# A fused two-block kernel: order of TensorE's work in the linear-attention mixer, by token tile

## The reference

```python
def gla_mixer(u, w_in, w_gk2, b_gk, g_norm, w_out):      # 4 heads, dk 128, dv 256, chunks of 64 tokens
    q, k, v, g, gk_lr = jnp.split(u @ w_in, [...], axis=-1)
    log_a = jax.nn.log_sigmoid((gk_lr @ w_gk2 + b_gk)) / GLA_GATE_TAU
    ...
    cum = jnp.cumsum(to_chunks(log_a, GLA_DK_HEAD), axis=3)
    e_pos = jnp.exp(cum)
    e_neg = jnp.exp(-cum)
    q_fwd = qc * e_pos
    a_fwd = jnp.einsum('bhntd,bhnsd->bhnts', q_fwd, kc * e_neg)
    a_bwd = jnp.einsum('bhntd,bhnsd->bhnts', qc * e_neg, kc * e_pos)
    o_intra = jnp.einsum('bhnts,bhnsv->bhntv', jnp.where(lower, a_fwd, a_bwd), vc)
    k_to_end = kc * jnp.exp(cum[:, :, :, -1:, :] - cum)
    chunk_decay = jnp.exp(cum[:, :, :, -1, :])

    def step(state, inp):
        qs, ke, vv, dec = inp
        o = jnp.einsum('bhtk,bhkv->bhtv', qs, state)
        state = state * dec[..., None] + jnp.einsum('bhtk,bhtv->bhkv', ke, vv)
        return state, o
    ...
    o = o_intra + o_inter
    o = o * lax.rsqrt(jnp.mean(jnp.square(o), -1, keepdims=True) + RMS_EPS) * g_norm
    return (o * jax.nn.silu(g)) @ w_out
```

## Time and profile before

| what | value |
|---|---|
| device time, median of 3 runs | 1047.37 us (1047.06 to 1048.85) |
| the profiled execution, device time | 1045.79 us |
| its span | 1043.8 us |
| its mean granted clock of TensorE | 0.992 |
| TensorE, VectorE, ScalarE busy | 97%, 62%, 19% of the span |
| bytes read from HBM | 203.64 MB, 196 GB/s over the span |

### The profile page before, as it was taken

The page is one execution under the profiler, slowest core; times in us unless marked ns, Lnnn a source line. Parts: engine busy times, 40 slices in busy tenths (PEclk is TensorE's granted clock), DMA queues, the critical chain, the costliest instruction groups (busy, mean ns, idle before and its releaser), DMA issues. The chain is left out here.

```text
span 1043.8 us, 12930 instructions
## 1 busy us (share of the span) xinstructions
PE 1010.2 (97%) x4878; PEld 712.5 (68%) x4880; DVE 652.4 (62%) x1533; ACT 203.1 (19%) x492; POOL 26.3 (3%) x53
## 2 busy tenths in 40 slices
PE   7999999999999999899999999999999999999994
PEld 4858755858755757656777777668886677777762
DVE  2786644785642341546899888975332577766668
ACT  4134214134212231202000000022223110001000
POOL 2000000000000000000001000001000000000000
PEclk9999999999999999999999999999999999999997
DMA  9954457754447355173669877825433345554411
GB/s 357 379 175 181 169 172 272 291 194 158 180 166 297 137 221 207 42 293 115 231 248 344 299 249 266 289 85 205 149 131 121 121 140 183 206 184 175 162 40 41
DMA packets 29909, 205.50 MB, mean 197 GB/s; under 512 B 3630, under 2 KB 3795, under 8 KB 6172
## 3 DMA queue, kind: packets, MB, share of 16 engines
q1 hardware_dynamic: 27116, 191.60, 50.4%
q0 software_dynamic: 2736, 13.11, 3.3%
HBM read 203.64 MB, written 1.05 MB: 196 GB/s over the span
## 5 line engine op out<-in xcount | busy, mean ns | idle before, releaser
L1503 PE MATMUL bank<-hT,raw 128*128 128x256 f32 x1056 | 235.1, 382 | 2.0 <-DMA raw<-units_dram 2.0
L1503 PEld LDWEIGHTS bank<-hT,raw 128*128 128x128 f32 x1056 | 200.1, 191 | 33.6 <-issue 3.8
L1792 PE MATMUL bank<-yT,arena 128*128 128x512 f32 x224 | 100.8, 593 | 0.0
L1792 PE MATMUL bank<-raw,arena 128*128 128x512 f32 x180 | 86.8, 593 | 0.0
L1792 PEld LDWEIGHTS bank<-yT,arena 128*128 128x128 f32 x224 | 42.5, 190 | 53.9 <-issue 51.7
L820 DVE CUSTOM_DVE_ANT_0 raw<-raw,crow 128x1024 f32<-128x1024 f32 x64 | 75.3, 1220 | 0.2 <-DVEq L118 0.2
L1816 PEld LDWEIGHTS bank<-hT,raw 128*128 128x128 f32 x448 | 54.3, 192 | 12.4 <-issue 12.4
L1513 PE MATMUL bank<-raw,hT 128*128 128x512 f32 x128 | 55.4, 592 | 0.0
L676 ACT ACTIVATE arena<-bank 128x512 f32<-128x512 f32 x28 | 16.7, 597 | 197.0 <-PE bank L1816 197.0
L1816 PE MATMUL bank<-hT,raw 128*128 128x128 f32 x448 | 54.5, 275 | 0.0
L1513 PE MATMUL bank<-raw,yT 128*128 128x512 f32 x112 | 49.5, 596 | 2.1 <-DVE yT L1432 2.0
(11 more groups left out here) (342 smaller groups left out, 1398.8 us busy)
## 6 DMA issues: line engine op xcount, KB each, us to landing
raw<-units_dram SPq DMA_DIRECT2D x180, 1024.0 KB, 4.8
arena<-ln_rows_dram POOLq DMA_DIRECT2D x4, 1024.0 KB, 5.5
arena<-att_line_dram POOLq DMA_DIRECT2D x4, 512.0 KB, 6.0
arena<-small_dram POOLq DMA_DIRECT2D x2, 896.0 KB, 7.1
arena<-ada_rows_dram POOLq DMA_DIRECT2D x1, 1536.0 KB, 8.0
xt<-x_dram SPq DMA_DIRECT2D x2, 512.0 KB, 4.5
arena<-post_g_dram POOLq DMA_DIRECT2D x2, 512.0 KB, 8.8
kst<-consts_dram SPq DMA_DIRECT2D x1, 608.0 KB, 15.9
```

The costliest lines, as they stand in the source:

```text
L1503: mm = pe.matmul(b[:, c * S:(c + 1) * S], raw[:, s, k * 256 + c * P:k * 256 + (c + 1) * P], act_t[:, k, :], start=(k == 0), stop=(k == KC ...
L1792: return pe.matmul(SB[i][:], x, y, start=False, stop=stop)
```

## The change

On TensorE alone, three things are done in the GLA mixer. The key transposes stand ahead of the scores. The waits ahead of the outputs are split by token tile: tile 0 waits for `st0_ready` 2 and `att_ready` 2, tile 1 for `att_ready` 4 and `st_ready` 8. And the output units wait apart: the first for `yg_ready` 4, the second for `yg_ready` 8. No instruction with work in it is added or removed, and the programs of the other engines are the same.

```diff
@@ -1921,6 +1921,11 @@
                 unit_t(0, N_GLA + GW_AT[8 + g], hT, G[g])
             pe.wait_ge(qkm_ready, 10)
 
+            for t in range(NT):
+                for h in range(H):
+                    mm = pe.transpose(G[2 + t][:, h * P:(h + 1) * P], ke[:, h, t * P:(t + 1) * P], ident)
+            mm.then_inc(kep_ready, 1)
+
             pe.wait_ge(vg_ready, 4)
             for t in range(NT):
                 c = slice(t * P, (t + 1) * P)
@@ -1928,11 +1933,6 @@
                     for h in range(H):
                         mm = pe.matmul(A[2 * t + i][:, h * P:(h + 1) * P], k[:, h, c], q[:, h, c], start=True, stop=True)
                 mm.then_inc(attp_ready, 1)
-
-            for t in range(NT):
-                for h in range(H):
-                    mm = pe.transpose(G[2 + t][:, h * P:(h + 1) * P], ke[:, h, t * P:(t + 1) * P], ident)
-            mm.then_inc(kep_ready, 1)
 
             pe.wait_ge(gate_ready, 2)
             pe.wait_ge(ken_ready, 2)
@@ -1945,9 +1945,12 @@
                                    vg[r, c // 2, h * S:(h + 1) * S], start=True, stop=True)
                 mm.then_inc(stp_ready, 1)
 
-            pe.wait_ge(att_ready, 4)
-            pe.wait_ge(st_ready, 8)
+            pe.wait_ge(st0_ready, 2)
             for t in range(NT):
+
+                pe.wait_ge(att_ready, 2 * t + 2)
+                if t == 1:
+                    pe.wait_ge(st_ready, 8)
                 for h in range(H):
                     o = A[2 * t + h // 2][:, (h % 2) * S:(h % 2 + 1) * S]
                     if t > 0:
@@ -1973,8 +1976,9 @@
                         mm = pe.transpose(G[q][:, i * S + t * P:i * S + (t + 1) * P],
                                           xs[:, t, (2 * q + i) * P:(2 * q + i + 1) * P], ident)
                 mm.then_inc(ogp_ready, 1)
-            pe.wait_ge(yg_ready, 8)
             for w in range(2):
+
+                pe.wait_ge(yg_ready, 4 * w + 4)
                 unit_n(0, N_GLA + GW_AT[12 + w], yT, G[2 * w:2 * w + 2], 0)
             n = N_GLA + GW_AT[14]
             for i in range(2):
```

## The result

The changed kernel takes 1039.91 us (median of 6 runs, 1039.0 to 1041.15) against 1047.13 us for the kernel before, measured anew beside it (6 runs, 1044.4 to 1048.85). The ratio is 0.9941 with a 95% interval of 0.9929 to 0.9954, so 4.8 to 7.4 us less. The forecast was 1041.0 us and 6.38 us less. The profiled execution took 1040.39 us with a span of 1038.4, where 1037.4 had been forecast.

What follows compares the result with a forecast made beforehand. TensorE, multiplying for 97% of the span, was taken as the bound, so only its idle or slow time counts. 1.26 + 1.84 + 1.71 + 1.57 = 6.38 us off 1047.37 gave 1041.0 us, range 1038.9 to 1043.6.

Steps and rivals of the forecast that it cites:

- Part 1: Key transposes ahead of the scores: the 1.26 us wait before state products L1944 goes, masks keeping 1.5 us of cover.
- Part 2: First tile's outputs wait for one state: the 1.84 us wait before L1959 goes; second tile has 1.9 us of cover.
- The clock: First tile's outputs: without idle time the granted clock no longer falls to 0.50; gain 1.71 us, bounds 0 and 3.4.
- The first rival: Half-width products, 417.0 to 430.7: the clock falls all the same, only waits are won, 4.67 us; 1042.7 us, chance 15%.
- stands between full-width work: The 1.98 us wait before output projection L1513: said to leave the clock at 1.00 because full-width work surrounds it.
- Part 3: First output unit L1513 waits for four of eight yT pieces: starts 1.57 us earlier, 0.4 us of idle time stays.
- more than one fall: Closing the 1.26 us wait also saves a clock fall that the profile does not have; 1039.3 us, chance 7%.
- What could give it back: Transposes L1973, VectorE's loads and two output takes, feed-forward start: claimed to lose nothing; loads move 4.8 us, TensorE 6.4.
- The second rival: Load of VectorE's unit at 466.58 does not move, its queue being full: 0.9 us lost, 1041.9 us, chance 5%.
- the slower one: Outputs L1959 to L1961 and L1954: continuous half-width work holds the clock down; 1051.1 us, chance 3%.
- The level: Whole-kernel time: 6.38 us off the earlier timed median of 1047.37 us, giving 1041.0 us.

Runs made afterwards that it cites:

- the filled wait: Kernel before, with eight 512-column bf16 products of zeros put into TensorE's 1.84 us wait ahead of the outputs; ratio 0.9990 (0.9976 to 1.0004).
- part 2 alone: Kernel before, with only the output waits split, so the first token tile's outputs wait for one state; ratio 0.9975 (0.9961 to 0.9989).
- part 1 alone: Kernel before, with only the key transposes moved ahead of the scores; ratio 1.0005 (0.9984 to 1.0026).
- part 3 alone: Kernel before, with only the first output unit waiting for four parts of yT instead of eight; ratio 0.9987 (0.9973 to 1.0001).
- parts 1 and 3: Changed kernel with the split of the output waits undone, so both tiles wait for all eight state sums; ratio to the kernel before 0.9978 (0.9966 to 0.9990).

## Why the prediction was right, step by step

- **Part 1, 1.26 us.** Right as a wait: from the first of transposes and scores to L1944 it was 5.88 us and is 4.54. The cover was there, 1.64 us where 1.5 had been worked out. What the working did not see is that this gain exists only together with part 2; alone, most of it was given back by a fall of twice the length (1.05 us more in the outputs).
- **Part 2, 1.84 us.** Right: L1962 follows the state products at once, and L1957 has no bracket. The last state sum ends at 423.24 + 1.66 = 424.90, and L1957 starts at 426.74: 1.84 us of cover where 1.9 had been worked out.
- **The clock, 1.71 us.** Right in its cause, which the filled wait and part 2 alone show together, and in its size within the profile (outputs of 3.61 us where 3.58 had been worked out). That the mean over many executions comes out near it as well, 1.5 ± 0.4 us, is partly luck. The forecast had one fall, in every execution; the runs have two, the other behind the wait before L1513, and neither comes every time. Where the outputs' fall alone is taken away (part 2, or the fill), 0.9 ± 0.5 and 1.0 ± 0.6 us less are forgone. The first rival, that the fall stays among half-width products, is refuted: none of the profiles in which that wait is gone or filled has a fall there. Its premise was misread too, in that nothing but half-width products would run until 430.7: L1954 in the earlier trace rows, L1957 now, is 128*128. The Trainium skill's rule on gaps between bursts ("TensorE: Matmul & The Clock Gate", section "Why this matters for your kernels"), by which these waits would have been too short to matter, does not hold here: the lower level follows waits of 1.84 and, in three profiles of four, 1.98 us, and the first of these falls goes away where its wait is filled.
- **One step of the reasoning was wrong**, though it cost little in the forecast: that the 1.98 us wait before L1513 "stands between full-width work" and so leaves the clock at 1.00. That was one execution. Profiles of part 1 alone, part 2 alone and the filled outputs' wait, with the same wait, have a fall there that costs 15.70 - 14.00 = 1.7 us. Part 3 is therefore worth 1.57 us and, in some executions, 1.7 us more. The rival "more than one fall" was right in kind, but had put the other fall behind the 1.26 us wait.
- **Part 3, 1.57 us.** 1.98 became 0.41 in the profile, exactly that; in part 3 alone the stage is 1.57 us shorter too. Over its ten executions it is 0.9 ± 0.4 us at full clock, not a contradiction but no sharp confirmation.
- **What could give it back.** Nothing did. The load for L1262 moved by 466.58 - 462.43 = 4.15 us against the 5.37 of TensorE's L1756, and the second take at L1139 kept its cover, as worked out. The second rival is out, and so is the slower one: 1.00 throughout.
- **The level.** 1039.91 instead of 1041.0. The 1.1 us are within the spread of such sets of runs (the medians of the kernel before went from 1045.76 to 1047.37); the fall behind L1513 that part 3 also takes away, and that the profile of before didn't have, goes the same way, but its share was not measured apart.

## What to carry to other kernels

A wait of TensorE can cost more than its length, since the products behind it may run at the lower clock; price a wait by its bracket and by the granted clock of the work behind it. Close such waits together rather than one by one; here the first one closed alone won nothing that could be told. If one cannot be closed, full-width products of zeros may be put into it: here they kept the clock up behind the 1.84 us wait and cost nothing at full clock (1034.4 to 1034.6 us, 1034.5 without them). And read the clock in more than one execution before saying that a place has none of it: where a fall comes in some executions only, the mean of span times clock, and of span times its complement, separates the two kinds of loss when single times do not.

## What was not expected of the hardware

- Taking 1.26 us of idle time out, ahead of a 1.84 us wait that stays, came with a longer low stretch: 3.4 us in the kernel before, 6.8 us with part 1 alone and with parts 1 and 3 (the 6 us rows above are at 0.50 throughout), one profile of each. It began before the outputs and lasted through nearly all of them. Why it came sooner and stayed longer was not settled.
- The same wait before L1513, 1.98 us, was followed by the lower level in three of the four profiles that had it unfilled and unshortened (part 1 alone, part 2 alone, outputs' wait filled), and not in that of the kernel before. With the wait shortened to 0.41 us or less, or filled, no profile has a fall there.
- Only part of what was expected of the falls shows in the means. The profiles have a fall in the outputs in five cases of five and one before L1513 in three of four, which would make some 3 us for the change; the sums give 1.5 ± 0.4. Falls in places that the change does not touch come and go from one execution to the next (six of the thirteen profiles have one in the first 31 us, both of the changed kernel among them, that of the kernel before not). Whether chance in these makes the difference was not settled.
